# Parameter vectors loaded as columns, and the forget gate taken out of the head of each layer

## The reference

```python
for l in range(DEPTH):
    h = rmsnorm(x, norm_mix_g[l])
    proj = h @ w_in[l]
    q, k, v, f_logit, cx, cb, cc, px, gate_logit = jnp.split(proj, IN_SPLITS, axis=-1)
    qh = rmsnorm(heads(q), q_norm_g[l])
    kh = rmsnorm(heads(k), k_norm_g[l])
    logf = log_sigmoid(f_logit + forget_b[l])      # 8 heads
    a = forgetting_attention(qh, kh, heads(v), logf)   # logits + (cumsum(logf)_q - cumsum(logf)_k)
    ...                                            # conv and pooling branches, gates, w_o, then the FFN
```

## Time and profile before

| | |
|---|---|
| median of 3 runs | 1769.64 us (1768.84 to 1773.84) |
| profiled execution, its time | 1769.52 us |
| its span | 1767.7 us |
| TensorE's mean granted clock | 0.963 |
| TensorE busy | 1667.1 us, 94% |
| VectorE busy | 1104.0 us, 62% |
| ScalarE busy | 816.6 us, 46% |
| first projection matmul | 22.12 us after the span's start |

### The profile page before, as it was taken

One profiled execution on the slowest core, in us unless ns is written; L12 is line 12 of the kernel. 1 busy time (PEld: TensorE's weight loads), 2 busy tenths in 40 slices (PEclk: granted clock), 3 DMA queues, 4 the chain that ended last, 5 costly groups with the idle time before them and its releaser, 6 DMA issues.

```text
span 1767.7 us, 29183 instructions
## 1 busy us (share of the span) xinstructions
PE 1667.1 (94%) x12312; PEld 1567.8 (89%) x12312; DVE 1104.0 (62%) x1380; ACT 816.6 (46%) x1067; POOL 107.1 (6%) x84
## 2 busy tenths in 40 slices
PE   5999899999899989999998999998999999899998
PEld 5989899998899989999887899997999999799997
DVE  5755667775575576877576566667756544255554
ACT  6444453444544435444567554445444434254442
POOL 1400000000130000000021000000111111000000
PEclk9999999999899999999998999999999999699999
DMA  6864456566566436666543356676765444135552
GB/s 213 289 207 158 131 170 226 200 230 238 170 234 217 160 108 205 215 227 205 181 136 99 105 181 237 238 250 204 261 215 191 148 143 158 30 119 170 189 191 96
DMA packets 229984, 324.57 MB, mean 184 GB/s; under 512 B 7237, under 2 KB 199390, under 8 KB 229342
## 3 DMA queue, kind: packets, MB, share of 16 engines
q1 hardware_dynamic: 219962, 313.21, 52.6%
q10 hardware_dynamic: 9892, 9.50, 1.7%
HBM read 313.24 MB, written 9.44 MB: 183 GB/s over the span
## 4 chain that ended last, share of the span: by engine, by line
PE 80%; issue 7%; DVE 6%; ACT 4%; POOL 1%; SPq 1%; DMA 0%; ACTq 0%; POOLq 0%; DVEq 0%
PE bank L467 24%; PE bank L468 23%; PE bank L469 23%; PE bank L508 2%; ACT whi L1024 2%; DVE wlo L1476 1%; POOL rstd L970 1%; PE bank L534 1%; PE bank L845 1%; PE bank L603 1%; PE bank L605 1%; PE bank L673 1%; PE bank L865 1%; PE bank L855 1%; SPq L918 1%
## 5 line engine op out<-in xcount | busy, mean ns | idle before, releaser
L1476 DVE TENSOR_TENSOR wlo<-raw,whi 128x2048 fp32r<-128x2048 f32 (+3 forms) x243 | 549.7, 2264 | 298.7 <-ACT whi L1024 298.6
L1024 ACT ACTIVATE whi<-raw 128x2048 fp32r<-128x2048 f32 (+3 forms) x243 | 458.3, 1888 | 138.0 <-PE bank L469 116.2
L467 PE MATMUL bank<-hT_hi,whi 128*128 128x256 f32 x1744 | 503.2, 289 | 0.8 <-issue 0.8
L468 PE MATMUL bank<-hT_lo,whi 128*128 128x256 f32 x1744 | 497.6, 285 | 0.0
L469 PE MATMUL bank<-hT_hi,wlo 128*128 128x256 f32 x1744 | 497.4, 285 | 0.0
L467 PEld LDWEIGHTS bank<-hT_hi,whi 128*128 128x128 f32 x1744 | 338.9, 194 | 8.0 <-issue 6.7
L468 PEld LDWEIGHTS bank<-hT_lo,whi 128*128 128x128 f32 x1744 | 339.0, 194 | 1.2
L469 PEld LDWEIGHTS bank<-hT_hi,wlo 128*128 128x128 f32 x1744 | 338.8, 194 | 0.0
L467 PE MATMUL bank<-whi,hT_hi 128*128 128x256 f32 (+1 forms) x944 | 276.5, 293 | 12.6 <-DVE qn L1578 5.9
L468 PE MATMUL bank<-wlo,hT_hi 128*128 128x256 f32 (+1 forms) x944 | 271.5, 288 | 0.0
L469 PE MATMUL bank<-whi,hT_lo 128*128 128x256 f32 (+1 forms) x944 | 271.3, 287 | 0.0
(11 more groups left out here) (264 smaller groups left out, 1626.8 us busy)
## 6 DMA issues: line engine op xcount, KB each, us to landing
raw<-in_mlp_w SPq DMA_DIRECT2D x64, 1024.0 KB, 5.5
ada_raw<-in_ada_w SPq DMA_DIRECT2D x96, 512.0 KB, 6.1
raw<-in_w_in SPq DMA_DIRECT2D x44, 1024.0 KB, 5.4
raw<-in_w_ffn_in SPq DMA_DIRECT2D x44, 1024.0 KB, 5.2
raw<-in_dil_w_in SPq DMA_DIRECT2D x36, 1024.0 KB, 5.1
raw<-in_w_ffn_out SPq DMA_DIRECT2D x22, 1024.0 KB, 4.9
raw<-in_w_o SPq DMA_DIRECT2D x8, 1024.0 KB, 5.2
bias_near<-near SPq DMA_DIRECT2D x2, 3072.0 KB, 10.3
```

The source lines that it names most:

```text
L467: pe.matmul(dst, lh, rh, start=start, stop=False)
L468: pe.matmul(dst, lh, rl, start=False, stop=False)
L1024: act.activation(view(whi[c % SPL], c), view(raw[c % RAW], c), ACT.Copy).then_inc(s_hi, 1)
L1476: dve.tensor_tensor(view(wlo[c % SPL], c), view(raw[c % RAW], c), view(whi[c % SPL], c).bitcast(F32), ALU.subtract).then_inc(s_lo, 1)
```

## The change

- The host lays the vectors out as `colA` and `colB`, and two DMAs from ScalarE's queue load them straight into place. The row tiles, their 26 loads, the transposes and the copies are gone.
- The forget weights become a tile of their own, `fw` (128 partitions of 8 x 8), with their own high and low halves, made in the middle of Q and K. F is no longer a chunk: Q0 is the first chunk, and TensorE computes F behind K1, into a bank of the other set.
- ScalarE does Abs and Exp behind V0's copy and the transposed K1, Ln behind V1's copy; VectorE does the subtraction and the scan behind V1's splits.
- The angles move from VectorE's very first work to behind V1's splits in layer 0, their Sin pair on ScalarE to behind CB's copy. Only the latent layer waits for them.
- x is loaded in two halves of 128 tokens. At the first norm VectorE squares the last quarter. SyncE loads `csil`, `pos_t` and `freq` behind K0, `causal` and `invcount` behind V1.
- Q0's matmuls go through the pairs of `hT` in the order in which they come, for both halves of the tokens.

```diff
+        fw, fw_hi, fw_lo = sb("fw", [P, DK, H1]), sb("fw_hi", [P, DK, H1], F32R), sb("fw_lo", [P, DK, H1], F32R)
...
-            chunk(("F", l), kmajor(w_in, F_AT, P))
...
-            pe.wait_ge(s_const, CONSTS)
-            pe.wait_ge(s_rows, 16 * N_ROWS_DMA)
-            bk = begin("w", "colA")
-            end(pe.transpose(bk[:, 0:NA_ROWS], rowA[:, :], ident[0:NA_ROWS, 0:NA_ROWS]), "colA")
-            bk = begin("w", "colB")
-            end(pe.transpose(bk[:, 0:NB_ROWS], rowB[:, :], ident[0:NB_ROWS, 0:NB_ROWS]), "colB")
+            pe.wait_ge(s_const, 16)
...
-                w = weights(("F", l))
-                bk = begin("w", ("F", l))
-                for k in range(DK):
-                    await_pair(("nrm", 2 * l), 0, k)
-                    m = mm3(bk[:, 0:S], w[0][:, k, :], w[1][:, k, :], hT_hi[:, k, :], hT_lo[:, k, :], k == 0, k == DK - 1)
-                end(m, ("F", l))
-                used(("F", l))
...
-                    token_major((nm, l, c), w, 0, 256, hT_hi, hT_lo, 0, DK)
+                    token_major((nm, l, c), w, 0, 256, hT_hi, hT_lo, 0, DK, first_of=None if i else ("nrm", 2 * l))
                     used((nm, l, c))
+                    if i == 3:
+                        pe.wait_ge(s_fwlo, l + 1)
+                        bk = begin("a", ("F", l))
+                        for k in range(DK):
+                            m = mm3(bk[0:H1, 0:S], fw_hi[:, k, :], fw_lo[:, k, :], hT_hi[:, k, :], hT_lo[:, k, :],
+                                    k == 0, k == DK - 1)
+                        end(m, ("F", l))
...
-            sp.dma_start(x[:, :, :], A["x"][0].rearrange("(t p) d -> p t d", p=P)).then_inc(s_x, 16)
+            for t in range(TT):
+                sp.dma_start(x[:, t, :], A["x"][0, P * t:P * t + P, :]).then_inc(s_x[t], 16)
...
-                if c == 1:
-                    sp.wait_ge(s_set0, 1)
-                    for dst, row in row_loads[N_ROWS_ACT:]:
-                        sp.dma_start(dst, row).then_inc(s_rows, 16)
+                if name == ("K", 0, 0):
+                    sp.dma_start(csil[:, :], A["c_2"][0:1, :].broadcast_to([P, D])).then_inc(s_cload, 16)
+                    sp.dma_start(pos_t[:, :], A["positions_2"][0].rearrange("(t p) -> p t", p=P), allow_slow_non_contiguous=True)\
+                      .then_inc(s_freq, 16)
+                    sp.dma_start(freq[:, :], A["freq"]).then_inc(s_freq, 16)
+                if name == ("V", 0, 1):
+                    sp.dma_start(causal[:, :], A["causal"]).then_inc(s_causal, 16)
+                    sp.dma_start(invcount[:, :, :], A["invcount"].rearrange("p (a s) -> p a s", a=2)).then_inc(s_inv, 16)
+                if name == ("Q", 1, 0):
+                    sp.wait_ge(s_fwlo, 1)
+                    sp.dma_start(fw[:, :, :], A["fw"][1]).then_inc(s_fw, 16)
...
-            pool.memset(rowB[:, :], 0.0).then_inc(s_set0, 1)
...
-            act.dma_start(pos_t[:, :], A["positions_2"][0].rearrange("(t p) -> p t", p=P), allow_slow_non_contiguous=True).then_inc(s_freq, 16)
-            act.dma_start(freq[:, :], A["freq"]).then_inc(s_freq, 16)
             act.dma_start(ident[:, :], A["ident"]).then_inc(s_const, 16)
-            act.dma_start(causal[:, :], A["causal"]).then_inc(s_const, 16)
-            act.dma_start(invcount[:, :, :], A["invcount"].rearrange("p (a s) -> p a s", a=2)).then_inc(s_const, 16)
-            act.dma_start(fb[:, :], A["forget_b"].rearrange("l h -> h l"), allow_slow_non_contiguous=True).then_inc(s_const, 16)
-            act.wait_ge(s_set0, 1)
-            for dst, src in row_loads[:N_ROWS_ACT]:
-                act.dma_start(dst, src).then_inc(s_rows, 16)
-            act.dma_start(csil[:, :], A["c_2"][0:1, :].broadcast_to([P, D])).then_inc(s_cload, 16)
+            act.dma_start(colA[:, :], A["colA"]).then_inc(s_cols, 16)
+            act.dma_start(colB[:, :], A["colB"]).then_inc(s_cols, 16)
+            act.dma_start(fw[:, :, :], A["fw"][0]).then_inc(s_fw, 16)
+            act.dma_start(fb[:, :], A["forget_b"].rearrange("l h -> h l"), allow_slow_non_contiguous=True).then_inc(s_cols, 16)
 
...
-                    for q in range(4):
+                    for q in range(4 if e else 3):
                         t, half = divmod(q, 2)
                         if e == 0:
-                            act.wait_ge(s_x, 16)
+                            act.wait_ge(s_x[t], 16)
...
-            split_ahead(("F", 0), 1)
-            full(act, "colA")
-            act.activation(colA[:, :], bank[jobs["colA"][2]][:, 0:NA_ROWS], ACT.Copy).then_inc(drain_sem("colA"), 1)
-            full(act, "colB")
-            act.activation(colB[:, :], bank[jobs["colB"][2]][:, 0:NB_ROWS], ACT.Copy).then_inc(drain_sem("colB"), 1)
+            split_ahead(("Q", 0, 0), 0)
+            act.wait_ge(s_cols, COLS)
...
-                emptied(act, "colA")
                 norm_high(2 * l, lambda k: colA[:, c_mix(l) + k:c_mix(l) + k + 1])
-                split_ahead(("F", l))
+                split_ahead(("Q", l, 0))
...
-                    act.wait_ge(s_ropein, 1)
-                    act.activation(cosn[:, :, :], ang[:, 4, :].rearrange("p (t f) -> p t f", t=TT), ACT.Sin).then_inc(s_rope, 1)
-                    act.activation(sinn[:, :, :], ang[:, 3, :].rearrange("p (t f) -> p t f", t=TT), ACT.Sin).then_inc(s_rope, 1)
-                    act.wait_ge(s_rope, 2)
-                act.wait_ge(s_z, l + 1)
-                link(act.activation(tf[:, :], zf[:, :], ACT.Abs))
-                link(act.activation(tf[:, :], tf[:, :], ACT.Exp, scale=-1.0))
-                act.activation(tf[:, :], tf[:, :], ACT.Ln, bias=1.0).then_inc(s_zt, 1)
...
+                    if i == 1:
+                        act.wait_ge(s_fw, 16 * (l + 1))
+                        if l:
+                            full(act, ("F", l - 1))
+                        act.activation(fw_hi[:, :, :], fw[:, :, :], ACT.Copy).then_inc(s_fwhi, 1)
...
+                        act.wait_ge(s_z, l + 1)
+                        link(act.activation(tf[:, :], zf[:, :], ACT.Abs))
+                        act.activation(tf[:, :], tf[:, :], ACT.Exp, scale=-1.0).then_inc(s_ac, 1)
+                        steps[0] += 1
+                    else:
+                        act.wait_ge(s_ac, steps[0])
+                        act.activation(tf[:, :], tf[:, :], ACT.Ln, bias=1.0).then_inc(s_zt, 1)
...
+                if l == 0:
+                    act.wait_ge(s_ropein, 1)
+                    act.activation(cosn[:, :, :], ang[:, 4, :].rearrange("p (t f) -> p t f", t=TT), ACT.Sin).then_inc(s_rope, 1)
+                    act.activation(sinn[:, :, :], ang[:, 3, :].rearrange("p (t f) -> p t f", t=TT), ACT.Sin).then_inc(s_rope, 1)
+                    act.wait_ge(s_rope, 2)
...
+                if ev == 0:
+                    dve.wait_ge(s_x[1], 16)
+                    link(dve.tensor_tensor_reduce(xn[:, 1, 512:], x[:, 1, 512:], x[:, 1, 512:], 1.0, 0.0, ALU.mult, ALU.add,
+                                                  sqs[:, 1, 1:2]))
+                    dve.wait_ge(s_ss, 3)
+                    dve.sem_inc(s_ss, 1)
...
+            def angles():
+                dve.wait_ge(s_freq, 32)
+                link(dve.tensor_copy(posf[:, :], pos_t[:, :]))
...
-                    split_ahead(("F", 0), 1)
-                    emptied(dve, "colA")
-                    emptied(dve, "colB")
+                    split_ahead(("Q", 0, 0), 0)
+                    dve.wait_ge(s_cols, COLS)
...
-                bk = full(dve, ("F", l))
-                dve.wait_ge(s_rope, 2)
-                dve.tensor_scalar(zf[:, :], bk[0:H1, 0:S], fb[:, l:l + 1], None, ALU.add).then_inc(drain_sem(("F", l)), 1)
-                emptied(dve, ("F", l))
-                link(dve.memset(zero1[:, :], 0.0))
-                dve.tensor_scalar(mf[:, :], zf[:, :], 0.0, None, ALU.min).then_inc(s_z, 1)
-                dve.wait_ge(s_zt, l + 1)
-
-                link(dve.tensor_tensor(mf[:, :], tf[:, :], mf[:, :], ALU.subtract))
...
+                    if i == 1:
+                        dve.wait_ge(s_fwhi, l + 1)
+                        dve.tensor_tensor(fw_lo[:, :, :], fw[:, :, :], fw_hi[:, :, :].bitcast(F32), ALU.subtract)\
+                           .then_inc(s_fwlo, 1)
                 for c in range(2):
                     finish_head_norm()
+                    if c == 0:
+                        bk = full(dve, ("F", l))
+                        dve.tensor_scalar(zf[:, :], bk[0:H1, 0:S], fb[:, l:l + 1], None, ALU.add)\
+                           .then_inc(drain_sem(("F", l)), 1)
+                        emptied(dve, ("F", l))
+                        link(dve.memset(zero1[:, :], 0.0))
+                        dve.tensor_scalar(mf[:, :], zf[:, :], 0.0, None, ALU.min).then_inc(s_z, 1)
                     split_ahead(("V", l, c))
+                if l == 0:
+                    angles()
+                dve.wait_ge(s_zt, l + 1)
+                link(dve.tensor_tensor(mf[:, :], tf[:, :], mf[:, :], ALU.subtract))
```

(46 more changed lines are left out.)

62 lines of the change are left out of this document (25 added, 37 removed).

## The result

The changed kernel takes 1749.37 us (median of 4 runs, 1748.6 to 1751.67), the kernel before 1769.24 in the runs beside it (1766.74 to 1773.84): 0.9887 of the time, interval 0.9864 to 0.9909. The forecast was 1758.0 and its range ended at 1753. The sign was right, and the gain is 20 us where 11.6 were summed.

What follows compares the result with a forecast made beforehand. TensorE, busy 94% of the span, was taken as the bound, so only its waits could be gained: 6.1 - 1.8 + 2.8 + 4.5 = 11.6 off 1769.5 gives 1757.9, rounded 1758.0 us; range 1753 to 1764.

Steps and rivals of the forecast that it cites:

- Step 1: Kernel start: 26 row loads, transposes and copies removed, so low `xn` is done by about 9.2 us instead of 13.6.
- Steps 2 and 3: Start: first query chunk landed at 9.3 us, first projection matmul at 16.0 instead of 22.12; 6.1 us gained.
- Step 4: Start: TensorE's first matmuls run at half rate for 3.4 us; 1.8 us lost.
- Step 5: Layer 0: with the softplus later, `qn` comes before Q1 ends; TensorE's wait of 2.8 us goes.
- Step 6: Layer 1: waits of 0.9 on `wlo` and 2.5 on `qn` go, with 1.1 of half rate; together 4.5 us.
- Step 7: Moved forget, softplus and angle work hides in idle time; cover before CC's low half 1.2 us in layer 0; no cost.
- The step that failed: Behind the start and the heads of layers 0 and 1, everything shifts as a block; no further gain or loss.
- clock terms: Half rate of TensorE: 1.8 us lost at the start, 1.1 gained behind the `qn` wait in layer 1.
- A: Start: first query chunk lands late, at 12.5 us, so the kernel takes 1761.1 us; chance 0.14.
- B: Layers 0 and 1: the waits on `qn` stay, gain only 5.2, so 1764.3 us; chance 0.10.
- C: VectorE gives CC's low half late: 1775 to 1778 us, chance 0.03 in full, 0.05 in part.

Runs made afterwards that it cites:

- the columns alone: The kernel before with the columns loaded by two DMAs; forget gate, softplus and angles stay where they were: 1766.18 us, ratio 0.9968.
- the filled pair: Both kernels with matmuls that nobody reads in seven of the norms' waits: kernel after 1750.78 us, kernel before 1764.0 us.
- the four offsets: The kernel after without delay and with its first loads held back by 1.2, 2.3 and 3.5 us: 1749.37, 1760.23, 1761.56 and 1754.36 us.
- the forget gate's return: The kernel after with the forget gate back at the head of each layer, as a small tile: 1759.71 us, ratio 0.9934.

## Why the prediction came out too high

**Step 1** (26 rows away, low `xn` by 9.2) was right: VectorE ends it at 9.2. But the row loads were only the last of several things that this wait was for. Alone, without the queries first, their removal moved the first matmul by 1.0 us, as the columns alone showed.

**Steps 2 and 3** were right, and the forecast a little too early: split at 9.91 for 9.3, first matmul at 16.42 for 16.0. Gained 5.7 for 6.1.

**Step 4**, the clock at the start, had its sign and place right and its size at -1.8; the rows give -1.1. The rate changed at about 18.9, earlier than the row I took it from.

**Step 5** was right, with a margin of 2.5 us where 1.8 were forecast. Start and layer 0 together: 5.7 - 1.1 + 2.8 = 7.4, with 7.7 measured at V0 and 7.1 forecast.

**Step 6**: the waits of 0.9 and 2.5 are gone. The clock's term, 1.1, was sized for the one stretch behind the wait on `qn`. The stretch behind the norm at 446, which the forecast let stand, went too: 15.1 - 8.0 = 7.1 us for 4.5, so that the clock's part is 3.7.

**Step 7** was right: no moved work became a wait, the cover is 1.7 us, and the table loads around the Sin pair cost TensorE nothing, though the one behind them delays ScalarE's first exponential by 1.3 us.

**The step that failed** is the sentence behind the sum, "Behind these places everything shifts as a block, because TensorE is the bound and its progress releases every load and split", and with it the clock's term of step 6. For the work the sentence holds over 1000 us. For the rate at which the work is done it doesn't: a shift of the start by 1.2 us, with no other change, was worth 11 us. In the two traces the forecast missed 19.8 - 11.6 = 8.2 us: 4.7 at the late places, where it had nothing, 2.6 at the head of layer 1, where the clock gave 3.7 for 1.1, 0.6 at the start and layer 0, and 0.3 between.

Without its clock terms the forecast had 6.1 + 2.8 + 0.9 + 2.5 = 12.3 us of waits. The corrected times differ by 1723.8 - 1710.5 = 13.3, the filled pair by 13.9, and the two traces alone, corrected in the same way, by 19.8 - 0.356 x 23 = 11.6. So the sum of the waits was right within what these runs can tell. The other 7.9 of the 21.1 us between the means (1770.9, of the kernel before's later executions, and 1749.8) are 22.3 us less at half rate, times 0.356.

With the delays taken off, the four offsets of the kernel after average 1754.5 and the three of the kernel before 1769.0. That is 14.5 us apart, with single pairs from 8 to 21. The measured 20 is the lucky end. The point forecast needed some 2 to 3 us more of gain, and the range had to reach some 5 us further down, to the pair with 21.

The Trainium skill, "TensorE: Matmul & The Clock Gate", Part 1, says that the number of matmuls that fall into the ramp differs from run to run, and that the ramp's penalty stays under 1% of a typical span. The ramp at the start of the kernel after agrees with the second, at 1.1 us or 0.06%. The whole time at half rate does not: 110 to 137 us, at 0.356 each, are 39 to 49 us or 2.2 to 2.8% of the span, and moving the start changed the mean from 1749.8 to 1761.5, by 0.7%. For a change worth 0.7% that is no small matter.

**The rivals.** A (the chunk late) and B (the waits on `qn` stay) didn't come, and of C (CC's low half late) there was no sign, at a cover of 1.7 us.

**What stays open.** Why the clock falls behind a given wait at one offset and not at the next was not settled; the runs show that it does. Why delays of 1.2 and 2.3 us bring stretches and one of 3.5 us takes most of them away is part of the same question. Of the 4.8 us of the forget gate's return 2.6 are located. No kernel tried had a lower median than the changed one, and among the four offsets its own is the fastest.

## What to carry to other kernels

When a change is worth about 1%, list the time at half rate for each execution beside its time, and run both kernels with their start held back by a microsecond or two: what stays is the change, and what moves with the offset is, in this case, the clock's part. A wait names only its last releaser, so before you price its removal follow each other input of the waiting instruction to its own end. Keep clock stretches out of the sum and put them into the range.
